# Nineteen of 32 expert groups in the choice stage of an attention and product-key layer, gates from unit 25, one dot a unit

## The chip, the cores and the metric

One core of one Trainium2 chip runs the whole layer. The metric is device time in microseconds (us) from one launch, the median of several runs.

## What is computed

The layer is a hybrid attention block followed by a product-key expert layer (PEER). The change touches the expert layer alone:

```python
T, D = 512, 2048                     # tokens, model width
PEER_HEADS, PEER_TOPK = 8, 16        # 128 chosen experts (slots) a token
q = (xt @ w_pq).reshape(T, PEER_HEADS, 2, PEER_HALF)
s = jnp.einsum('thcd,hcnd->thcn', q, sub_keys)
s1, i1 = lax.top_k(s[:, :, 0], PEER_TOPK)
s2, i2 = lax.top_k(s[:, :, 1], PEER_TOPK)
...
idx = jnp.take_along_axis(cidx, pos, axis=-1)     # 8 x 16 of 16384 experts
g = jax.nn.softmax(top_s, axis=-1)
h = jax.nn.gelu(jnp.einsum('ted,td->te', u[idx], x))
out = jnp.einsum('te,ted->td', g * h, v[idx])
```

All in float32; the tables u and v hold 16384 rows of 2048 numbers each (128 MB a table).

## The kernel before

**Two ways to the same sum.** For tokens 0 to 383 (three blocks, `DB` = 3) the kernel doesn't gather. It multiplies all 16384 rows of u with the tokens, sets to zero by a table of gates what was not chosen, and multiplies with all of v. The last token block (128 tokens, block 3) is computed row by row: for each of its 128 slots one gather of u rows (1 MB, one row a partition), a dot product on the vector engine, later one gather of v rows and one multiply-add (`dot`, L1596, and `add_row`, L1617). The last 48 tokens of block 2 are half and half: their u side is made by 48 gathers and dots (`pair_dot`, L1494: 32 for the last 32 tokens, then 16 for the 16 tokens before them), so the u matmuls have only 336 columns (`UT`), and their v side is dense.

**Units.** Weights come in pieces of 1 MB, called units. For each the DMA queue of SyncE (SP) loads `raw` (`load`, L391), ScalarE (ACT) rounds it to `wh` (`split_hi`, L399), VectorE (DVE) subtracts to get the rest `wl` (`lo`, L1128), and TensorE (PE) multiplies three times, high with high, high with low, low with high (L419 to L421 for u, L444 to L446 for v). There are two buffers of each. The PE's next unit waits for its `lo`; the `split_hi` of unit k waits until PE has finished unit k-2; so `lo` of a unit can start some 2.5 us into the unit before it, and has to be done when that one ends.

**Stages.** The 16384 experts are 32 groups of 4 units of u and 4 units of v (v is cut otherwise, by output columns).
- *Choice stage*: the u units of the first `LAG` = 17 groups, 68 units of index k = 0 to 67. Their results go through gelu to a scratch tensor in DRAM (`act_scratch`, L631), since the gates don't exist yet. Beside these matmuls DVE looks up which experts were chosen (`lookup`, three operations, L1433 to L1440), and from unit `GATE_FROM` = 16 on PE makes the gates: two batches a unit, 96 in all, between the matmuls of the unit (`gate_batch`, L1970), from one-hot tiles that DVE (`hot`, L1456 and L1469) or, for every fourth batch up to number 80, ACT (`rows_act`, L1038 and L1043) has made. ACT copies the batches into `gate_piece` (L1063), and after every eighth SP stores that tile, 2 MB, to DRAM (L662). There is one such tile, so the next copy waits for the store. Each `rows_act` stands behind such copies in ACT's order. The 48 `pair_dot` stand at the units of `DOT_UNITS`; the gather of dot j+2 is issued by GpSimd (POOL, L797) when dot j is done, since there are two row buffers.
- *Main stage*: `NMAIN` = 15 groups with their 4 units of u and then a group's 4 units of v. A group has 5 or 6 slots of block 3 (`SLOT_COUNTS`), each with its dot and its add, and three row buffers: the gather of row n is issued when row n-3 is used (`gather_used`).
- *Tail*: the v units of the other 17 groups, one group alone (set 0) and then eight sets of two groups, 8 units a set. The activations and gates of these groups are read back (L668, L672), multiplied (`gate_mult`, L1584) and split (`tail_w_act` on ACT, L1085, and `tail_rest` on DVE, L1589). The slots of block 3 that are left, 1 and then 5 in each of eight sets, are worked off here.

**Order.** Nothing schedules at run time: each engine's order is written by hand in the loops below, where `for k in range(...)` walks the units. Within a tail set DVE's order is fixed by the source; the adds of the set before are split over two places:

```python
tail_lo(q, 1)
for j in before[:2]:
    add_row(s - 1, j)
tail_lo(q, 2)
gate_mult(NMAIN + 2 * q + 1)
for j in before[2:]:
    add_row(s - 1, j)
dot(s, 0)
tail_chunk(q, 0)
tail_lo(q, 3)
```

`before` is slots 2 and up of the set before (slots 0 and 1 were added at its end), and `tail_chunk` adds a finished output piece from PSUM (L468).

The last 48 tokens' dots come back into the gates by way of `pair_weights` (L1504 and L1509, at unit `DOT_UNITS[-1] + 3`) and a transpose on PE ahead of unit `PAIR_TURN` (`turn_pair`, L1960).

Of the kernel before, what the change touches and what calls it, by code (L numbers as in the profile page):

```python
# [47 lines left out]
GRP = 4  # L48
NGRP = NKEYS // GRP
CH = D // 512  # L50
LAG = 17
DB = TB - 1
TD = DB * P
PT = 32
PB = 16
UT = TD - PT - PB
FULL = UT // 32
PQ = P // PT
NMAIN = NGRP - LAG
GT = 32  # L60
NGC = TD // GT
GATE_FROM = 16
GATE_STEP = 2
GATE_UNITS = DB * 32 // GATE_STEP
GATE_PARTS = (2, 5)
LOOK_ORDER = (2, 0, 1, 3)
LOOK_AT = {1: GATE_FROM, 3: GATE_FROM + 38}
TURN_AT = (13, GATE_FROM + 12, GATE_FROM + 28)
PAIR_TURN = GATE_FROM + 40
GM = 6  # L70
SLOTS = PH * TOPK
PN = SLOTS // PQ
# [1 line left out]
assert GATE_STEP == 2  # L74
QB = P // PB
NB = SLOTS // QB
DOT_UNITS = sorted([8, 9, 11, 12, 13, 14, 15] + list(range(20, 39)) + list(range(21, 38, 3)) +
                   list(range(40, 52)) + list(range(42, 52, 3)))
assert len(DOT_UNITS) == PN + NB and DOT_UNITS[PN - 1] == 38 and DOT_UNITS[PN] == 40
assert GATE_FROM == 16 and UT % 16 == 0 and FULL == UT // GT and PAIR_TURN < GATE_FROM + (SLOTS - PB - PT) // 4 + 32  # L80
EPS = 1e-6
SQ_ACT = (0, 2, 3)
SCALE = float(HD) ** -0.5
# [8 lines left out]
N_PRO = N_PQ + 2 * PH  # L92
N_MAIN = N_PRO + GRP * LAG
N_TAIL = N_MAIN + 2 * GRP * NMAIN
N_END = N_TAIL + GRP * LAG
N_PROUNITS = GRP * LAG
LO_DVE = N_PRO + 4
# [4 lines left out]
M_PRO = M_PQ + 2 * PH  # L102
M_MAIN = M_PRO + GRP * LAG

# [4 lines left out]
FC = 40  # L109
TAIL_SETS = [(0,)] + [(_r, _r + 1) for _r in range(1, LAG, 2)]  # L110
SET_START = [sum(CH * len(_q) for _q in TAIL_SETS[:_n]) for _n in range(len(TAIL_SETS))]
# [28 lines left out]
def build(nc, x, attn_g, w_f, w_in, b_forget, q_g, k_g, w_out, ffn_g, ffn_row, w_pq, sub_keys, u, v, u_rows,  # L140
          v_rows, out):
    ctx = ExitStack()
    with ctx:
# [979 lines left out]
        def _(dve):  # L1123
# [302 lines left out]
            def lookup(t, c, half):  # L1426

                s0 = t * P + 64 * half
                look3 = look.rearrange("p (s j) -> p s j", j=TOPK)
                look4 = look.rearrange("p (h k j) -> p h k j", h=PH // 2, k=TOPK)  # L1430
                if t == DB:
                    dve.wait_ge(slots_turned, 1)
                picked(nc.vector.tensor_tensor(  # L1433
                    look3, pos2f[c][:, s0:s0 + 64].unsqueeze(2).broadcast_to([P, 64, TOPK]),
                    iota16[:].unsqueeze(1).broadcast_to([P, 64, TOPK]), ALU.is_equal))
                picked(nc.vector.tensor_tensor(
                    look4, look4.bitcast(F32),
                    idx_f[:, t, 4 * half:4 * half + 4, c, :].unsqueeze(2).broadcast_to([P, PH // 2, TOPK, TOPK]),
                    ALU.mult))
                nc.vector.tensor_reduce(slots[t][:, c, 64 * half:64 * half + 64], look3.bitcast(F32), AX.X,  # L1440
                                        ALU.add).then_inc(slots_done, 1)
                dve.wait_ge(slots_done, 4 * LOOK_ORDER.index(t) + 2 * c + half + 1)
# [92 lines left out]
            for k in range(8, GATE_FROM):  # L1535
                lo(N_PRO + k + 1)
                if k < 12:
                    lookup(0, (k - 8) // 2, (k - 8) % 2)
                if k == TURN_AT[0]:
                    take_slots(0)  # L1540
                for j, at_unit in enumerate(DOT_UNITS):
                    if at_unit == k:
                        pair_dot(j)
            hot(0)
            hot(1)
            for k in range(GATE_FROM, N_PROUNITS):
                ahead = GATE_STEP * (k - GATE_FROM) + 2
                lo(N_PRO + k + 1)
                if ahead < DB * 32:
                    hot(ahead)  # L1550
                for t in (1, DB):
                    if LOOK_AT[t] <= k < LOOK_AT[t] + 4:
                        lookup(t, (k - LOOK_AT[t]) // 2, (k - LOOK_AT[t]) % 2)
                for j, at_unit in enumerate(DOT_UNITS):
                    if at_unit == k:
                        pair_dot(j)
                if k == 20:
                    dve.wait_ge(side_chosen, 16 * QB)
                    nc.vector.memset(p_h[P // 2:P - PT], 1.0).then_inc(side_one, 1)
                if k == DOT_UNITS[-1] + 3:  # L1560
                    pair_weights()
                if ahead + 1 < DB * 32:
                    hot(ahead + 1)
                for t in range(1, DB):
                    if k == TURN_AT[t]:
                        take_slots(t)
                if k == PAIR_TURN:
                    take_pair()
                if k == LOOK_AT[DB] + 4:
                    nc.vector.scalar_tensor_tensor(out=g_idx[:], in0=slots[DB][:, 0, :], scalar=float(NKEYS),  # L1570
                                                   in1=slots[DB][:, 1, :], op0=ALU.mult,
                                                   op1=ALU.add).then_inc(chosen_done, 1)
                if k == GATE_FROM + GATE_UNITS:
                    nc.vector.memset(stat[:, 15:16], 0.0).then_inc(choice_done, 1)
# [512 lines left out]
```

## Time and profile before

| | us |
|---|---|
| median of 3 runs | 3251.55 (3249.18 to 3255.22) |
| the profiled execution, its own time | 3252.24 |
| its span, first to last instruction | 3250.5 |
| mean granted TensorE clock | 0.998 |
| PE busy | 3216.1 (99%) |
| DVE busy | 2263.4 (70%; 87% in the main stage, 83% in the tail) |
| ACT, POOL busy | 1119.1, 933.6 |
| choice stage | 1153 to 1756 |
| main stage | 1756 to 2691 |
| tail | 2691 to 3247 |

The span is the time between the first and the last recorded instruction, 1.7 us less than the execution's own time. Times in rows are counted from the span's start. A page of the profile gives the busy time of each engine, and a matmul's mean there overlaps with its neighbours; the pace of PE is read from the starts of instructions. An idle time in brackets at the end of a timeline row is that of the row's engine just before it, with the instruction or transfer that ended it.

### The profile page before, as it was taken

To read this page: it belongs to the slowest core of one execution; us is meant where nothing else is said; L and a number is where in the kernel's file an instruction comes from. 1 tells how busy PE (TensorE), PEld (TensorE's weight loads), DVE (VectorE), ACT (ScalarE), POOL (GpSimd) and SP (SyncE) were. 2 spreads that over 40 slices of the span, in tenths; PEclk is the share of its full clock that TensorE was granted. 3 is DMA by queue.
4 is the path that set the end of the run, shared out by engine and by line. 5 is a ranking of instruction groups with operands and counts; after the bars stand their busy time and mean duration, and the time that the engine had idled before them with its cause. 6 is when DMAs were issued, how large, how long until landed. Compare 5 with 4: busy or idle time off the path is not lost. (4 is left out here: it accounts for less than half of the span.)

```text
span 3250.5 us, 41510 instructions
## 1 busy us (share of the span) xinstructions
PE 3216.1 (99%) x16730; PEld 2818.6 (87%) x16730; DVE 2263.4 (70%) x2636; ACT 1119.1 (34%) x1172; POOL 933.6 (29%) x424
## 2 busy tenths in 40 slices
PE   8999999999999999999999999999999999999999
PEld 6878778887878899999999899889989988888887
DVE  5666541113027888887874888888889888888887
ACT  5232323334232233655553223223222322222221
POOL 4333333333434321111101323223322321223222
PEclk9999999999999999999999999999999999999999
DMA  3222222223233247889877989999989998888888
GB/s 144 78 78 90 77 78 78 78 78 141 92 116 121 88 161 255 304 316 318 311 243 265 352 333 352 336 341 345 358 332 335 350 343 312 320 336 340 343 319 317
DMA packets 171364, 777.87 MB, mean 239 GB/s; under 512 B 14064, under 2 KB 80752, under 8 KB 86384
## 3 DMA queue, kind: packets, MB, share of 16 engines
q1 hardware_dynamic: 127488, 457.77, 38.6%
q0 software_dynamic: 43776, 318.79, 26.3%
q8 instruction: 60, 0.98, 0.1%
q14 instruction: 40, 0.33, 0.0%
HBM read 731.10 MB, written 44.34 MB: 239 GB/s over the span
## 5 line engine op out<-in xcount | busy, mean ns | idle before, releaser
L419 PE MATMUL bank<-xh,wh 128*128 128x336 f32 (+1 forms) x3184 | 1105.8, 347 | 1.6 <-DVE wl L1128 1.6
L421 PE MATMUL bank<-xh,wl 128*128 128x336 f32 (+1 forms) x3184 | 1090.1, 342 | 0.0
L420 PE MATMUL bank<-xl,wh 128*128 128x336 f32 (+1 forms) x3184 | 1088.2, 342 | 0.0
L399 ACT ACTIVATE wh<-raw 128x2048 fp32r<-128x2048 f32 x344 | 658.0, 1913 | 999.0 <-PE bank L446 723.3
L1128 DVE TENSOR_TENSOR wl<-raw,wh 128x2048 fp32r<-128x2048 f32 x252 | 576.8, 2289 | 215.2 <-ACT wh L399 214.9
L419 PEld LDWEIGHTS bank<-xh,wh 128*128 128x128 f32 x3184 | 599.3, 188 | 46.5 <-issue 3.8
L420 PEld LDWEIGHTS bank<-xl,wh 128*128 128x128 f32 x3184 | 599.5, 188 | 44.7 <-issue 1.9
L421 PEld LDWEIGHTS bank<-xh,wl 128*128 128x128 f32 x3184 | 598.2, 188 | 45.1
L405 POOL TENSOR_TENSOR wl<-raw,wh 128x2048 fp32r<-128x2048 f32 x92 | 424.9, 4618 | 739.5 <-ACT wh L399 739.5
L444 PE MATMUL bank<-wh,xh 128*128 128x512 f32 x1072 | 417.1, 389 | 0.8 <-DVE stat L1302 0.8
L446 PE MATMUL bank<-wh,xl 128*128 128x512 f32 x1072 | 417.0, 389 | 0.0
L445 PE MATMUL bank<-wl,xh 128*128 128x512 f32 x1072 | 417.0, 389 | 0.0
L811 POOL DMA_INDIRECT arena<-in_u_rows,g_idx x128 | 249.3, 1947 | 456.2 <-DVE acc L1617 224.5
L811 POOL DMA_INDIRECT arena<-in_v_rows,g_idx x128 | 179.2, 1400 | 605.3 <-DVE acc L1617 317.3
L1596 DVE CUSTOM_DVE_ANT_0 arena<-arena 128x2048 f32<-128x2048 f32 x128 | 291.9, 2288 | 54.9 <-DMA arena<-in_u_rows,g_idx 54.8
L1617 DVE SCALAR_TENSOR_TENSOR acc<-arena,acc 128x2048 f32<-128x2048 f32 x128 | 300.5, 2347 | 3.5 <-DMA arena<-in_v_rows,g_idx 0.2
L444 PE MATMUL bank<-wh,gh 128*128 128x512 f32 x720 | 280.6, 390 | 1.6 <-DVE wl L1128 1.6
L446 PE MATMUL bank<-wh,gl 128*128 128x512 f32 x720 | 280.3, 389 | 0.0
L445 PE MATMUL bank<-wl,gh 128*128 128x512 f32 x720 | 280.2, 389 | 0.0
L444 PEld LDWEIGHTS bank<-wh,xh 128*128 128x128 f32 x1072 | 201.2, 188 | 42.8 <-DVE stat L1302 1.0
L445 PEld LDWEIGHTS bank<-wl,xh 128*128 128x128 f32 x1072 | 201.2, 188 | 41.8
L446 PEld LDWEIGHTS bank<-wh,xl 128*128 128x128 f32 x1072 | 201.2, 188 | 41.6
(211 smaller groups left out, 2803.3 us busy)
## 6 DMA issues: line engine op xcount, KB each, us to landing
raw<-in_u SPq DMA_DIRECT2D x128, 1024.0 KB, 5.8
raw<-in_v SPq DMA_DIRECT2D x128, 1024.0 KB, 6.2
raw<-in_w_in SPq DMA_DIRECT2D x56, 1024.0 KB, 4.8
gate_scratch<-arena SPq DMA_DIRECT2D x12, 2048.0 KB
arena<-gate_scratch SPq DMA_DIRECT2D x32, 768.0 KB, 9.0
raw<-in_w_out SPq DMA_DIRECT2D x16, 1024.0 KB, 4.9
raw<-in_w_pq SPq DMA_DIRECT2D x16, 1024.0 KB, 4.9
act_scratch<-arena SPq DMA_DIRECT2D x68, 168.0 KB, 4.4
```

The lines of the kernel that those rows point to most:

```text
L399: nc.scalar.activation(wh[s][:], raw[s][:], ACT.Copy).then_inc(hi_done, 1)
L405: nc.gpsimd.tensor_tensor(wl[s][:], raw[s][:], wh[s][:].bitcast(F32), ALU.subtract).then_inc(lo_done, 1)
L419: nc.tensor.matmul(dst, w_h[:, c], xh[:, c, 0:width], start=(c == 0), stop=False)
L420: nc.tensor.matmul(dst, w_h[:, c], xl[:, c, 0:width], start=False, stop=False)
L421: last = nc.tensor.matmul(dst, w_l[:, c], xh[:, c, 0:width], start=False, stop=(c == KC - 1))
L444: nc.tensor.matmul(bank[:], a_hi(e)[:, rows_], w_h[:, e], start=begin, stop=False)
L445: nc.tensor.matmul(bank[:], a_hi(e)[:, rows_], w_l[:, e], start=False, stop=False)
L446: mm = nc.tensor.matmul(bank[:], a_lo(e)[:, rows_], w_h[:, e], start=False, stop=end)
L811: nc.gpsimd.indirect_dma_start(out=rows_g[n % ROW_BUFS], out_offset=None, in_=table, in_offset=bass.IndirectOffsetOnAxis(ap=g_idx[:, slot: ...
L1128: nc.vector.tensor_tensor(wl[k % 2][:], raw[k % 2][:], wh[k % 2][:].bitcast(F32), ALU.subtract).then_inc(lo_done, 1)
L1596: nc.vector.tensor_tensor_reduce(out=rows_g[b], in0=rows_g[b], in1=x_tok, scale=1.0, scalar=0.0, op0=ALU.mult, op1=ALU.add, accum_out=dots ...
L1617: nc.vector.scalar_tensor_tensor(out=acc[:, DB, :], in0=rows_g[b], scalar=dots[:, GM + j:GM + j + 1], in1=acc[:, DB, :], op0=ALU.mult, op1 ...
```

## The change

`LAG` becomes 19, so the choice stage has 76 units and the main stage 13 groups; the tail has set 0 and nine sets of two groups. `GATE_FROM` becomes 25, so the gates are made in units 25 to 72 instead of 16 to 63, with three units behind them instead of four. The lookup of block 1 moves to units 14 to 17, ahead of the gates. `DOT_UNITS` is another list: 16 dots before unit 25 (units 18, 21 and 24 have two), then one in each of units 25 to 43 but 30, 36 and 42, and one in each of 45 to 61 but 52. From `LAG` follow the slots: 76 in the main stage, 1 in set 0, then 6 in each of six tail sets and 5 in each of three.

```diff
-LAG = 17
+LAG = 19
...
-GATE_FROM = 16
+GATE_FROM = 25
...
-LOOK_AT = {1: GATE_FROM, 3: GATE_FROM + 38}
+LOOK_AT = {1: 14, 3: GATE_FROM + 38}
...
-DOT_UNITS = sorted([8, 9, 11, 12, 13, 14, 15] + list(range(20, 39)) + list(range(21, 38, 3)) +
-                   list(range(40, 52)) + list(range(42, 52, 3)))
+DOT_UNITS = sorted([8, 10, 12, 13, 14, 16, *range(18, 25), 18, 21, 24] +
+                   [_k for _k in range(25, 44) if _k not in (30, 36, 42)] +
+                   [_k for _k in range(45, 62) if _k != 52])
...
                 if k < 12:
                     lookup(0, (k - 8) // 2, (k - 8) % 2)
+                if LOOK_AT[1] <= k < LOOK_AT[1] + 4:
+                    lookup(1, (k - LOOK_AT[1]) // 2, (k - LOOK_AT[1]) % 2)
...
-                for t in (1, DB):
-                    if LOOK_AT[t] <= k < LOOK_AT[t] + 4:
-                        lookup(t, (k - LOOK_AT[t]) // 2, (k - LOOK_AT[t]) % 2)
+                if LOOK_AT[DB] <= k < LOOK_AT[DB] + 4:
+                    lookup(DB, (k - LOOK_AT[DB]) // 2, (k - LOOK_AT[DB]) % 2)
...
-                if k == 20:
+                if k == GATE_FROM + 4:
```

In the changed file lines from 1541 on stand two higher and those from 80 to 1540 one higher.

**DVE ahead of the first gate batch**: before (units 14 and 15, then the one-hot tiles of batches 0 and 1); `L1494` is a dot, whose second row reads its sum.

```order
L1128 TENSOR_TENSOR wl<-raw,wh 128x2048
L1494 ISA acc,arena<-acc 128x2048
L1494 ISA arena 128x1
L1128 TENSOR_TENSOR wl<-raw,wh 128x2048
L1494 ISA acc,arena<-acc 128x2048
L1494 ISA arena 128x1
L1456 TENSOR_TENSOR gh<-iota,arena 128x512
L1464 TENSOR_SCALAR arena<-arena 128x128
```

The same place in the changed kernel (units 23 and 24):

```order
L1129 TENSOR_TENSOR wl<-raw,wh 128x2048
L1495 ISA acc,arena<-acc 128x2048
L1495 ISA arena 128x1
L1129 TENSOR_TENSOR wl<-raw,wh 128x2048
L1495 ISA acc,arena<-acc 128x2048
L1495 ISA arena 128x1
L1495 ISA acc,arena<-acc 128x2048
L1495 ISA arena 128x1
L1457 TENSOR_TENSOR gh<-iota,arena 128x512
L1465 TENSOR_SCALAR arena<-arena 128x128
```

The last unit ahead of the gates now has two dots in front of the first one-hot tile, where it had one.

**DVE in a tail set**, from the `lo` of its second unit to that of its fourth: before.

```order
L1128 TENSOR_TENSOR wl<-raw,wh 128x2048
L1617 SCALAR_TENSOR_TENSOR acc<-arena,acc 128x2048 x2
L1128 TENSOR_TENSOR wl<-raw,wh 128x2048
L1584 TENSOR_TENSOR arena<-arena 128x4x12x32
L1617 SCALAR_TENSOR_TENSOR acc<-arena,acc 128x2048
L1596 ISA arena<-arena 128x2048
L1596 ISA arena 128x1
L468 TENSOR_TENSOR acc<-bank,acc 128x3x512
L1128 TENSOR_TENSOR wl<-raw,wh 128x2048
```

And in the changed kernel, in tail sets 2 to 7 (whose set before has 6 slots):

```order
L1129 TENSOR_TENSOR wl<-raw,wh 128x2048
L1619 SCALAR_TENSOR_TENSOR acc<-arena,acc 128x2048 x2
L1129 TENSOR_TENSOR wl<-raw,wh 128x2048
L1586 TENSOR_TENSOR arena<-arena 128x4x12x32
L1619 SCALAR_TENSOR_TENSOR acc<-arena,acc 128x2048 x2
L1598 ISA arena<-arena 128x2048
L1598 ISA arena 128x1
L469 TENSOR_TENSOR acc<-bank,acc 128x3x512
L1129 TENSOR_TENSOR wl<-raw,wh 128x2048
```

Between two `lo` there is one more add; the third row that is `lo` has to be done before the same end of a unit as before.

**SP at the end of the choice stage**: before, from the last store of gates to the first loads for the main stage.

```order
L662 DMA gate_scratch<-arena 128x32x128
L391 DMA raw<-in_u 128x2048
L631 DMA act_scratch<-arena 128x336
L391 DMA raw<-in_u 128x2048
L631 DMA act_scratch<-arena 128x336
L668 DMA arena<-act_scratch 128x4x336
L672 DMA arena<-gate_scratch 128x1536
L391 DMA raw<-in_u 128x2048
```

And in the changed kernel:

```order
L663 DMA gate_scratch<-arena 128x32x128
L392 DMA raw<-in_u 128x2048
L632 DMA act_scratch<-arena 128x336
L669 DMA arena<-act_scratch 128x4x336
L673 DMA arena<-gate_scratch 128x1536
L392 DMA raw<-in_u 128x2048
```

One load and one store of results stand between the last store of gates and the read of it, where two pairs stood: it is one unit nearer to the main stage.

## Rows read from the trace of the kernel before

**Rows 1.** The page: busy us of each engine, share of the span, instructions.

```profile
PE 3216.1 (99%) x16730; PEld 2818.6 (87%) x16730; DVE 2263.4 (70%) x2636; ACT 1119.1 (34%) x1172; POOL 933.6 (29%) x424
```

**Rows 2.** Timeline of ACT in the choice stage, the gelu at each unit's start (start, us, engine, line).

```profile
1634.62 0.45 ACT L1029 ACTIVATE arena<-bank 128x336 f32<-128x336 f32 x1 [1.15 <-PE bank L421]
...
1741.32 0.45 ACT L1029 ACTIVATE arena<-bank 128x336 f32<-128x336 f32 x1 [5.11 <-PE bank L421]
1748.68 0.45 ACT L1029 ACTIVATE arena<-bank 128x336 f32<-128x336 f32 x1 [4.38 <-PE bank L421]
```

**Rows 3.** Timeline of PE: where it waited between the choice stage's first gate and the main stage.

```profile
1276.55 0.49 PE L1970 MATMUL bank<-arena,gh 128*128 128x128 f32 x2 [0.36 <-ACT arena L1043]
...
1408.57 0.85 PE L1970 MATMUL bank<-arena,gh 128*128 128x128 f32 x3 [3.00 <-ACT arena L1043]
...
1521.38 0.49 PE L1970 MATMUL bank<-arena,gh 128*128 128x128 f32 x2 [0.78 <-ACT arena L1043]
...
1562.10 0.79 PE L1970 MATMUL bank<-arena,gh 128*128 128x128 f32 x3 [3.43 <-ACT arena L1043]
...
1764.95 0.41 PE L419 MATMUL bank<-xh,wh 128*128 128x336 f32 x1 [1.58 <-DVE wl L1128]
```

**Rows 4.** One stretch by engine: busy us (instructions), then PE's granted clock, DMA share, GB/s.

```profile
1408.80:1412.20 3.40, 3.40 (x15) 3.40 (x15) 1.52 (x1) 3.40 (x4) 0.00 (x0) 0.50 0.31 123
```

**Rows 5.** Timelines of SP, POOL and ACT around two stores of gates.

```profile
1388.40 0.39 SPq L662 DMA_DIRECT2D gate_scratch<-arena  x1
1430.56 0.39 SPq L662 DMA_DIRECT2D gate_scratch<-arena  x1
...
1385.72 0.94 POOL L797 DMA_INDIRECT acc<-in_u_rows,arena  x1 [0.30 <-issue]
...
1403.88 2.05 ACT L1063 ACTIVATE arena<-bank 128x512 f32<-128x512 f32 x2 [7.96 <-DMA gate_scratch<-arena]
1440.12 2.13 ACT L1063 ACTIVATE arena<-bank 128x512 f32<-128x512 f32 x2 [2.65 <-DMA gate_scratch<-arena]
```

**Rows 6.** Timeline of DVE after unit 15's dot: the first tile of batch 0.

```profile
1272.81 0.69 DVE L1456 TENSOR_TENSOR gh<-iota,arena 128x512 fp32r<-128x512 f32 x1
```

**Rows 7.** Timelines of DVE and ACT at unit 55: the pair's weights, and the unit's gelu.

```profile
1645.34 0.29 DVE L1509 TENSOR_TENSOR arena<-arena 64x128 f32<-64x128 f32 x1
...
1643.79 0.45 ACT L1029 ACTIVATE arena<-bank 128x336 f32<-128x336 f32 x1 [4.96 <-PE bank L421]
```

**Rows 8.** Timelines of POOL, SP and ACT ahead of the main stage.

```profile
1739.96 0.26 POOL L804 MEMSET arena<- 128x192 f32 x1 [131.02 <-DMA gate_scratch<-arena]
...
1742.29 0.37 SPq L668 DMA_DIRECT2D arena<-act_scratch  x1
...
1760.51 1.92 ACT L399 ACTIVATE wh<-raw 128x2048 fp32r<-128x2048 f32 x1 [4.01 <-DMA raw<-in_u]
```

**Rows 9.** Timeline of DVE in the fifth two-group tail set.

```profile
2990.47 4.80 DVE L1617 SCALAR_TENSOR_TENSOR acc<-arena,acc 128x2048 f32<-128x2048 f32 x2
...
2999.88 2.35 DVE L1617 SCALAR_TENSOR_TENSOR acc<-arena,acc 128x2048 f32<-128x2048 f32 x1
3003.51 2.29 DVE L1596 CUSTOM_DVE_ANT_0 arena<-arena 128x2048 f32<-128x2048 f32 x1 [1.28 <-DMA arena<-in_u_rows,g_idx]
...
3005.72 1.75 DVE L468 TENSOR_TENSOR acc<-bank,acc 128x1536 f32<-128x1536 f32 x1
3007.39 2.28 DVE L1128 TENSOR_TENSOR wl<-raw,wh 128x2048 fp32r<-128x2048 f32 x1
```

**Rows 10.** PE, POOL at that place; the last row is from the chain of waits.

```profile
3010.11 0.39 PE L444 MATMUL bank<-wh,xh 128*128 128x512 f32 x1
...
2984.50 3.00 POOL L811 DMA_INDIRECT arena<-in_v_rows,g_idx  x1 [7.27 <-DVE acc L1617]
...
2993.08 3.00 POOL L811 DMA_INDIRECT arena<-in_u_rows,g_idx  x1 [4.34 <-DVE acc L1617]
...
2519.17 11.07 DMA arena<-in_u_rows,g_idx
```

More of the change, by code:

```diff
@@ L76 @@
 NB = SLOTS // QB
-DOT_UNITS = sorted([8, 9, 11, 12, 13, 14, 15] + list(range(20, 39)) + list(range(21, 38, 3)) +
-                   list(range(40, 52)) + list(range(42, 52, 3)))
-assert len(DOT_UNITS) == PN + NB and DOT_UNITS[PN - 1] == 38 and DOT_UNITS[PN] == 40
-assert GATE_FROM == 16 and UT % 16 == 0 and FULL == UT // GT and PAIR_TURN < GATE_FROM + (SLOTS - PB - PT) // 4 + 32
+DOT_UNITS = sorted([8, 10, 12, 13, 14, 16, *range(18, 25), 18, 21, 24] +
+                   [_k for _k in range(25, 44) if _k not in (30, 36, 42)] +
+                   [_k for _k in range(45, 62) if _k != 52])
+assert len(DOT_UNITS) == PN + NB and DOT_UNITS[PN - 1] == 43 and DOT_UNITS[PN] == 45
+assert UT % 16 == 0 and FULL == UT // GT and DOT_UNITS[-1] + 3 < PAIR_TURN <= GATE_FROM + 40
 EPS = 1e-6
```

## The prediction, made before the changed kernel ran

> **What bounds the kernel now.** I read the page first: PE is busy for 99% of the span [rows 1], so time can come and go only where PE waits or runs at another pace. The number of matmuls of each shape is the same before and after: two groups move from the main stage to the tail, their u units to the choice stage, and the 96 gate batches stay 96. So I looked for pace and for waits. The pace is even: from the gelu of one unit to the next it is 1748.68 - 1741.32 = 7.36 us for a u unit without gates [rows 2] and 1643.79 - 1634.62 = 9.17 us with two gate batches [rows 2, 7]; neither price changes when a unit moves. The waits are few [rows 3]: at the gate batches PE was idle for 0.36, 3.00, 0.78 and 3.43 us because ACT's rows (L1043) were late, and for 1.58 us in the second main unit because `lo` was. After the wait of 3.00 us PE's granted clock was 0.50, the lower of its two levels (1.2 of 2.4 GHz), for 3.4 us [rows 4]; half of that, 1.7 us, is lost on top. I take the same behind the wait of 3.43.
>
> Why was ACT late? At unit 28 SP issued a store of gates at 1388.40, and ACT could make its next copy at 1403.88, 15.5 us later, after 7.96 us of idling; the next store took 1440.12 - 1430.56 = 9.6 us and PE did not wait [rows 5]. Units 27 and 28 have three dots, so a gather had just been issued (1385.72) and others followed [rows 5]. With 15.5 us PE was idle for 3.00, so a store of up to some 12.5 us is hidden.
>
> **The change, part by part.**
>
> *One dot a unit: minus 10.6.* Since a dot's end issues the next gather, single dots 9.17 us apart leave at most one gather before a store and one during it, as around the store of 9.6 us (units 31 to 33). No store should pass 12.5 us then. What goes: 3.00 + 1.7, 3.43 + 1.7 and 0.78 = 10.6 us [rows 3, 4]. Bounds: 9 (a stall of one or two us stays) to 11.
>
> *The first gate: plus 5.0.* Batch 0 needs the tile that DVE makes behind the last dot. From that point (1272.81) to PE's batch (1276.55) it took 3.74 us, ACT's rows in between, and it came 0.36 too late [rows 3, 6]. Now unit 24 has two dots ahead of it. `lo` starts 2.5 us into the unit, behind gelu (0.45) and `split_hi` (1.92) [rows 2, 8], and takes 2.3, a dot takes 3005.72 - 3003.51 = 2.2 [rows 9], so DVE is free 9.2 us after the unit's start and batch 0 ready at 12.9; it is due at 7.36 + 2.8 (18 matmuls) = 10.2. Idle: 2.7 us at the least. The last dot's gather also has to come: it is issued when the dot of unit 23 ends (7.0 us into it), and from a gather's issue to its use pass 8.4 to 11.1 us (tail, below), which makes that dot 1.0 to 3.7 us later. I take 2.7 + 1.0 = 3.7, with the clock's 1.7, less the 0.36 of before: 5.0. Bounds: 2.3 (no late gather, no lower clock) and 7.7. The lookups moved to units 14 to 17 cost nothing: block 0's stand in the same way with `lo` and dots in units 8 to 11, before and now, and PE did not wait there.
>
> *The pair's weights: plus 1.2.* They are made in the unit `DOT_UNITS[-1] + 3`: before 54, while the transpose stands ahead of unit 56; now 64, with the transpose ahead of unit 65. Before, DVE had them at 1645.34 + 0.29 = 1645.6, and unit 55 had begun 0.35 us before its gelu, at 1643.4: 2.2 us earlier [rows 7]. Two units' room hid that. Now PE waits; the batch made in unit 64 is one whose rows ACT makes, so DVE has four small one-hot operations less ahead of the weights, by my guess 1 us. Bounds 1.0 and 2.2; I take 1.2.
>
> *The way into the main stage: plus 2.* The main stage's first loads wait for the last store of gates (POOL sees it at 1739.96), then read activations and gates (1742.29) and only then fetch the second main unit, which reached ACT at 1760.51, 20.5 us after the store; that made the wait of 1.58 [rows 3, 8]. The store is now one unit of 7.36 us nearer, so the wait could become 9 us. Against that, SP's read was held until 1742.29 by the result of unit 65, 2.3 us behind the store, and now isn't; and it comes level with POOL's first three gathers instead of behind them. Bounds minus 0.3 and plus 7.4; I take 2, nearer the low end because the read now leads. The Trainium skill (DMA: Bandwidth & Descriptors, Queues, rings and completion order) says that a DMA engine takes turns between queues packet by packet, so that neither SP's read nor POOL's gathers would block the other; by that rule the early read loses little and this term would be 0.5, the sum 1.5 lower. No row shows the turns.
>
> *The tail: plus 18.* This is the costly part. `LAG` = 19 leaves 51 slots for nine sets, and six have 6 where all had 5. The sixth adds a dot and an add. Two slots' adds come at the end of a set and two behind the second unit's start, so the additional add stands between the `lo` of the third and of the fourth unit, in six sets. In the fifth set of two groups of before, this stretch ended with the `lo` at 3007.39 + 2.28 = 3009.67, and PE began the next unit at 3010.11: 0.44 us of room [rows 9, 10]. The dot before it had waited 1.28 us for its gather. An add costs 2.27 us more in a row of adds (two take 4.80, overlapping by their ends [rows 9]). Without any wait for a gather: 3009.67 - 1.28 + 2.27 = 3010.66, so PE is some 0.6 to 0.8 us late. With it: the first dot of a set uses the row buffer freed by the slot three before, which with 6 slots is the add ending at 2990.47 + 4.80 = 2995.27 [rows 9]. Its gather is issued behind that of 2993.08, which keeps POOL for 3.00, so at 2996.4 [rows 10]. From issue to use passed 3003.51 - 2993.08 = 10.4 us here and 11.07 in the densest place of the main stage; and at most 8.4 where the add in the pair from 2990.47 on used the gather of 2984.50 without a wait [rows 9, 10]. With 10.4 the dot starts at 3006.8, and then 3009.67 - 3003.51 = 6.2 us follow: 3013.0, 2.9 us late. With 11.07 it is 3.6, and 4.1 if the adds before slip too; with 8.4 the adds decide and it is 0.8. Since every set's first `lo` is tied to PE by its `split_hi`, the lateness comes anew in each set: six times. I take 3.0, by the row of this very place: 18 us; bounds 6 x 0.7 = 4 and 6 x 4.1 = 25. Main groups with 6 slots show that the pattern stands more elsewhere: there `dot`s are spread over five units.
>
> *At nothing:* the end of the main stage now has a group with 6 slots ahead of set 0, with one add more before the second `lo`; I find 1 us of room left by the same walk. The 3 MB of `acc` read back for blocks 0 to 2 are issued behind unit 65's store and have three units until the next. The 2 us of small waits for gathers in the main stage stay.
>
> **Sum:** -10.6 + 5.0 + 1.2 + 2 + 18 = +15.6 us. The profiled execution's own time was 3252.2, 0.7 above the median 3251.55; the sum is put on the median: **3267**.
>
> **Rivals.**
> - *The clock goes down in the tail too (3277).* With 3 us each, the tail's waits are about as long as those of 3.00 us, behind which the granted clock was 0.50 [rows 3, 4]. Six times 1.7 is 10 more. For it: the length. Against: most of the six would have to reach it, and my bounds begin at 0.7. The Trainium skill (TensorE: Matmul & The Clock Gate, HAM oscillation) describes just this, idle stretches inside a loop that put PE back to 1.2 GHz time after time.
> - *Gathers come in time in the tail (3254).* With some 8.4 us from issue to use the tail costs 0.8 a set: 5 instead of 18, so +2.6. For it: the dots of the other tail sets did not hold up their `lo`, and the gathers that matter are issued at the same points as before. Against: the waiting dot of [rows 9].
> - *Faster (3244).* DVE's room covers the add, so the tail costs nothing; the first gate costs its least (2.3), the pair 1.0, the way into the main stage 0: -10.6 + 3.3 = -7.3. It decides whether one add fits between the two `lo`: 2.27 against 0.44 + 1.28 = 1.72 us. It misses by 0.55, by rows of a single set.
> - *The stores stay slow (3278).* Single dots still put gathers ahead of a store, because with two buffers there is nearly always one under way, and the stalls of 10.6 us stay. Against: the 9.6 us store had single dots around it.
>
> **How the numbers follow.** Chances: my sum 0.52, the clock 0.18, slow stores 0.08, gathers in time 0.14, faster 0.08. A measurement of this kernel tells about 0.2% (6.5 us) from no change. The first three are slower by more than that: 0.78. Gathers in time is within it: 0.14. The last is faster: 0.08. All lower bounds together give 3248, all upper ones 3285, and they won't fall together; the range is 3252 to 3284, which leaves out the faster case, the lower part of the fourth, and the upper part of the second.
>
> **What would show it.** In the choice stage no wait of PE on L1043 beyond the first gate, and there one of about 4 us; no wait of ACT on the gate store above 4 us before unit 61. A wait of a bit over 1 us at the transpose of the pair (L1962 in the changed file). In the second main unit a wait of 2 to 5 us. In the tail six waits of about 3 us on `lo`, 65 us apart plus the wait, behind a dot that waited for u rows. I am wrong if the tail stays without waits, or if the stores still take 15 us.

## The result: 1.0% slower, twice what was forecast

| | before | after |
|---|---|---|
| median of 5 runs, us | 3252.73 (3249.18 to 3258.18) | 3285.26 (3283.3 to 3288.97) |
| ratio, 95% interval | 1 | 1.010 (1.0086 to 1.0114) |
| profiled execution, its own time | 3252.24 | 3285.26 |
| its span | 3250.5 | 3283.5 |
| mean granted TensorE clock | 0.998 | 0.994 |

The forecast was 3267, with a range to 3284: the direction is right, the time 1.3 us outside the range, and the loss 32.5 us instead of 15.6.

The page of the changed kernel, the line of [rows 1] and three groups of instructions (busy, mean ns | idle before, releaser):

```profile
PE 3227.1 (98%) x16730; PEld 2824.9 (86%) x16730; DVE 2259.8 (69%) x2631; ACT 1120.1 (34%) x1171; POOL 927.9 (28%) x424
...
L445 PE MATMUL bank<-wh,xh 128*128 128x512 f32 x1168 | 460.1, 394 | 27.1 <-DVE wl L1129 26.3
...
L1598 DVE CUSTOM_DVE_ANT_0 arena<-arena 128x2048 f32<-128x2048 f32 x128 | 291.4, 2288 | 67.9 <-DMA arena<-in_u_rows,g_idx 67.7
L1619 DVE SCALAR_TENSOR_TENSOR acc<-arena,acc 128x2048 f32<-128x2048 f32 x128 | 300.6, 2349 | 9.6 <-DMA arena<-in_v_rows,g_idx 6.1
```

The same 16730 matmuls are busy 11 us longer (the granted clock is lower, see below), and the v units waited 26.3 us for `lo` (27.1 us is all the idle time before these matmuls). Where, the timeline of PE shows; first the three waits outside the tail that answer to [rows 3], then all six of the tail:

```profile
1345.84 0.88 PE L1972 MATMUL bank<-arena,gh 128*128 128x128 f32 x3 [3.67 <-ACT arena L1044]
...
1713.51 0.33 PE L1962 MATMUL bank<-ident,arena 128*128 128x128 f32 x1 [0.97 <-DVE arena L1510]
...
1817.91 0.42 PE L420 MATMUL bank<-xh,wh 128*128 128x336 f32 x1 [1.03 <-DVE wl L1129]
...
2747.17 0.80 PE L445 MATMUL bank<-wh,xh 128*128 128x512 f32 x1 [4.45 <-DVE wl L1129]
...
2819.56 0.79 PE L445 MATMUL bank<-wh,xh 128*128 128x512 f32 x1 [4.43 <-DVE wl L1129]
...
2890.44 0.50 PE L445 MATMUL bank<-wh,xh 128*128 128x512 f32 x1 [3.25 <-DVE wl L1129]
...
2960.80 0.80 PE L445 MATMUL bank<-wh,xh 128*128 128x512 f32 x1 [4.76 <-DVE wl L1129]
...
3033.09 0.79 PE L445 MATMUL bank<-wh,xh 128*128 128x512 f32 x1 [5.27 <-DVE wl L1129]
...
3105.51 0.79 PE L445 MATMUL bank<-wh,xh 128*128 128x512 f32 x1 [4.10 <-DVE wl L1129]
```

The places are those of the forecast: the first gate (3.67), the pair (0.97), the second main unit (1.03, before 1.58), and six times the fourth unit of a tail set, 26.3 us in all. The waits of 3.00, 0.78 and 3.43 at the gates [rows 3] are gone. The duration in the second column tells the clock: five of the six matmuls behind a wait show 0.79 or 0.80 us, the one behind 3.25 shows 0.50. The stretches behind those waits (PE, weight load, DVE, ACT, POOL busy; then the granted clock, as in [rows 4]):

```profile
2745.40:2752.20 6.80, 5.03 (x12) 3.97 (x13) 6.80 (x4) 0.00 (x0) 0.00 (x0) 0.51 0.95 348
2817.00:2823.80 6.80, 4.24 (x10) 3.37 (x11) 6.80 (x5) 0.13 (x1) 0.00 (x0) 0.51 0.90 317
2886.80:2893.60 6.80, 3.55 (x16) 2.61 (x15) 6.80 (x4) 1.91 (x1) 0.92 (x1) 1.00 0.97 365
2960.40:2963.80 3.40, 3.00 (x7) 2.42 (x8) 3.40 (x3) 0.00 (x0) 0.00 (x0) 0.52 0.99 361
3032.10:3038.90 6.80, 5.81 (x14) 4.55 (x15) 6.80 (x4) 0.00 (x0) 0.00 (x0) 0.51 0.95 373
3103.80:3110.60 6.80, 5.09 (x12) 4.02 (x13) 6.80 (x4) 0.00 (x0) 0.00 (x0) 0.51 0.93 359
```

In the five stretches at 0.51 or 0.52 (1.2 of 2.4 GHz) PE was busy for 5.03 + 4.24 + 3.00 + 5.81 + 5.09 = 23.2 us; half of that, 11.6, is what the clock cost.

A table of stage lengths, from the starts of each unit's last matmul, is used below. The columns are units; without a wait, unit 25 takes 9.17 us, the 56 units 195 to 250 take 457.0 and the rest 40.8. (The kernels with an e are the experiments of the next section.) Each row is a single execution.

| profiled execution | unit 25 | 26 to 64 | 65 | 77 | 78 to 194 | 195 to 250 | rest |
|---|---|---|---|---|---|---|---|
| after | 14.69 | 358.4 | 10.69 | 8.67 | 917.1 | 496.1 | 40.8 |
| e1 sixth add and dot behind `lo` | 19.73 | 358.4 | 10.69 | 8.40 | 915.7 | 459.6 | 45.6 |
| e9 only the dot behind `lo` | 17.27 | 358.4 | 10.68 | 9.45 | 916.7 | 457.2 | 40.8 |
| e4 sixth add on 64 columns | 20.54 | 358.4 | 10.68 | 9.26 | 920.1 | 495.7 | 41.0 |
| e2 four sets of six | 16.17 | 358.4 | 10.67 | 8.43 | 918.2 | 483.9 | 40.8 |
| e5 dots and pair moved | 9.79 | 358.4 | 9.29 | 11.24 | 919.2 | 497.9 | 42.2 |
| e11 only the dot of unit 24 moved | 9.78 | 358.4 | 10.69 | 9.44 | 917.5 | 496.9 | 41.9 |
| e8 e1 and e5, and the last set | 9.79 | 358.4 | 9.29 | 9.31 | 917.8 | 459.0 | 40.8 |
| e12 e8 with the pair late | 9.79 | 358.4 | 10.69 | 9.36 | 918.8 | 458.4 | 40.8 |
| e10 e8 with doubled dots | 11.19 | 371.8 | 9.29 | 9.75 | 918.7 | 459.2 | 40.8 |

Before, units 195 to 250 took 457.0. The tail alone is +39.1.

### The profile page after: what moved, and what is told of

Read it like the earlier page. It is cut to its first block and busy times, and to the rows that moved or that the text cites. A ratio compares the mean times of both kernels' runs of the same rounds, so it can differ in the third digit from the quotient of the medians.

```text
span 3283.5 us, 41419 instructions
## 1 busy us (share of the span) xinstructions
PE 3227.1 (98%) x16730; PEld 2824.9 (86%) x16730; DVE 2259.8 (69%) x2631; ACT 1120.1 (34%) x1171; POOL 927.9 (28%) x424
## 5 line engine op out<-in xcount | busy, mean ns | idle before, releaser
L445 PE MATMUL bank<-wh,xh 128*128 128x512 f32 x1168 | 460.1, 394 | 27.1 <-DVE wl L1129 26.3
L446 PE MATMUL bank<-wl,xh 128*128 128x512 f32 x1168 | 458.6, 393 | 0.0
L447 PE MATMUL bank<-wh,xl 128*128 128x512 f32 x1168 | 458.3, 392 | 0.0
L812 POOL DMA_INDIRECT arena<-in_u_rows,g_idx x128 | 227.1, 1775 | 419.6 <-DVE arena L1598 222.2
L445 PEld LDWEIGHTS bank<-wh,xh 128*128 128x128 f32 x1168 | 222.2, 190 | 75.9 <-DVE wl L1129 28.8
L446 PEld LDWEIGHTS bank<-wl,xh 128*128 128x128 f32 x1168 | 222.1, 190 | 46.4
L447 PEld LDWEIGHTS bank<-wh,xl 128*128 128x128 f32 x1168 | 221.8, 190 | 46.7
L445 PE MATMUL bank<-wh,gh 128*128 128x512 f32 x624 | 243.4, 390 | 0.5 <-DVE wl L1129 0.3
L447 PE MATMUL bank<-wh,gl 128*128 128x512 f32 x624 | 242.9, 389 | 0.0
L446 PE MATMUL bank<-wl,gh 128*128 128x512 f32 x624 | 242.9, 389 | 0.0
```

The lines of the kernel that those rows point to most:

```text
L445: nc.tensor.matmul(bank[:], a_hi(e)[:, rows_], w_h[:, e], start=begin, stop=False)
L446: nc.tensor.matmul(bank[:], a_hi(e)[:, rows_], w_l[:, e], start=False, stop=False)
L447: mm = nc.tensor.matmul(bank[:], a_lo(e)[:, rows_], w_h[:, e], start=False, stop=end)
L812: nc.gpsimd.indirect_dma_start(out=rows_g[n % ROW_BUFS], out_offset=None, in_=table, in_offset=bass.IndirectOffsetOnAxis(ap=g_idx[:, slot: ...
```

## The experiments

Each was compared with the kernel before on its own chip; the medians of before were 3250.9 (e1 to e4), 3252.0 (e5, e6, e8, e9) and 3253.96 (e10 to e12), so across these groups the ratios count.

**e3: before with LAG = 19 alone.** It separates the split of the groups from the gates and dots.

```diff
-LAG = 17
+LAG = 19
```

> The kernel before with LAG = 19 alone: gates from unit 16 and the old list of dots stay. Theory (the changed list gives 11 us in the choice stage, and its two new waits, at the first gate and at the pair's transpose, take 6.3): the tail's 39 us are there, the two waits at ACT's rows are back, the new ones are not, and the last store of gates is far from the main stage, whose first wait goes too: 3252 + 39 - 2 = 3289, some 4 us above the changed kernel. Rival (the choice stage's list makes the tail's waits, through the phase of the gathers): no waits in the tail, about 3250.

Measured 3289.3, ratio 1.0115 (1.0098 to 1.0132). Units 195 to 250 took 496.5 us, 39.5 over, as in the changed kernel (39.1). `LAG` makes the whole loss. Whether the gates and dots take a little of it back can't be told: the intervals of the two ratios overlap, and the profiles are 4.1 us apart. The old list's stalls were there again, but at units 30 and 34 (9.4 us together) instead of 30 and 46.

**e2: four sets of six instead of six.** Two of the 51 tail slots go to the main stage.

```diff
-SLOT_COUNTS = [GM - (_r % 5 == 4) for _r in range(NMAIN)]
+SLOT_COUNTS = [GM for _r in range(NMAIN)]
```

> The changed kernel, with 6 slots in every group of the main stage, so that four tail sets have 6 slots instead of six. Theory (each tail set behind one with 6 slots costs some 6.5 us): four waits instead of six, 13 us less, 3272, and nothing more than 1 us in the main stage. Rival (all tail sets cost, by more traffic): the same time, 3285, or more, since the main stage becomes denser by two slots and its two waits of about 1 us become four.

Measured 3278.63, ratio 1.0089 (1.0072 to 1.0106). Units 195 to 250: 483.9, so four sets cost 26.9 us, 6.7 each, where six cost 39.1, 6.5 each. The four sets behind six slots had a wait, and sets 6 and 7, now behind five, had none: the cost goes with the number of sets behind six slots, as forecast. The time shows less of it: by the ratios (1.0089 against 1.0100) 3.6 us of the 12.2 that the stage shows, with intervals that overlap, and not the 3272 that I expected; in the profile unit 25 took 1.5 and the main stage 1.1 us more.

**e1: the sixth add and the set's first dot behind `lo`.**

```diff
-                for j in before[2:]:
+                late = len(before) > 3
+                for j in before[2:3] if late else before[2:]:
                     add_row(s - 1, j)
-                dot(s, 0)
+                if not late:
+                    dot(s, 0)
                 tail_chunk(q, 0)
                 tail_lo(q, 3)
+                if late:
+                    add_row(s - 1, before[3])
+                    dot(s, 0)
```

> The changed kernel, with the sixth add of the set before and the first dot moved behind the lo of the fourth unit, in the six tail sets whose set before has 6 slots. Theory (the added time is the tail's: a lo that stands behind a waiting dot is late, six times 3.4 to 5.4 us of waiting, and the lower clock behind each): the dot's wait for its gather, some 3.5 us, now falls where the next lo is not due for 9 us, so none of the six waits is left, the clock stays up, and all 39 us go: 3246, about 6 us below the kernel before. Rival (the tail's gathers are short of bandwidth, and where they wait is a matter of place): the waits move to the lo of the fifth unit and 10 to 30 us stay.

Measured 3253.52 (10 runs), ratio 1.0008 (0.9998 to 1.0017): some 30 us of the loss are gone, and it is still 7 us above the 3246 that I expected. The six waits disappeared (the 56 units are 2.6 us over the undisturbed length); 4.8 us came up in a new place, the fourth unit of the last set (the rest took 45.6 instead of 40.8 us), where two dots stand ahead of that `lo`. Unit 25 was 5 us longer than in the changed kernel's profile, with the same code.

**e4 and e9: the add or the dot?** My sum went by the dot's gather; its lower bound, and the rivals "gathers in time" and "faster", went by the add's own time. e4 makes the sixth add small (64 of 2048 columns, the others of that row are left out) and changes nothing in the order.

```diff
+                cols = slice(0, 64 if r > NMAIN and j == 5 else D)
-                nc.vector.scalar_tensor_tensor(out=acc[:, DB, :], in0=rows_g[b],
-                                               scalar=dots[:, GM + j:GM + j + 1], in1=acc[:, DB, :],
+                nc.vector.scalar_tensor_tensor(out=acc[:, DB, cols], in0=rows_g[b][:, cols],
+                                               scalar=dots[:, GM + j:GM + j + 1], in1=acc[:, DB, cols],
```

> The changed kernel, with the sixth add of a tail set on 64 of 2048 columns (the output of the last token block is short of it); its gather is unchanged. Theory A (the late gather of the first dot decides; it is issued when the add two places ahead ends, so the sixth add's own 2.3 us lie inside the dot's wait of 3.3 to 3.8 us): the waits of PE stay within 0.3 us of what they were, the dot waits 2.2 us longer, total within 2 us of 3285. Theory B (my prediction's lower bound: the vector engine's own time decides): each of the six waits is 2.2 us shorter and the clock drops less, 13 to 25 us faster.

One execution, 3297.4. That is neither figure, but the stage table tells the two theories apart: units 195 to 250 took 495.7 us, 0.4 less than in the changed kernel (theory A). The 12 us more lie outside the edit: 5.9 in unit 25, 2.3 ahead of the choice stage, some 3.6 in units 77 to 194, 0.6 ahead of unit 25. DVE in its second such set:

```profile
2817.59 2.35 DVE L1620 SCALAR_TENSOR_TENSOR acc<-arena,acc 128x2048 f32<-128x2048 f32 x1
2820.60 0.28 DVE L1620 SCALAR_TENSOR_TENSOR acc<-arena,acc 128x64 f32<-128x64 f32 x1 [0.67 <-DMA arena<-in_v_rows,g_idx]
2825.89 2.29 DVE L1598 CUSTOM_DVE_ANT_0 arena<-arena 128x2048 f32<-128x2048 f32 x1 [5.00 <-DMA arena<-in_u_rows,g_idx]
```

The add took 0.28 us instead of 2.35, and the dot behind it waited 5.00 us for its gather where it had waited 3.26 in the changed kernel. So the add's duration is not on the path; the dot's row is.

e9 moves the dot alone, and leaves the whole sixth add ahead of `lo`:

```diff
                 for j in before[2:]:
                     add_row(s - 1, j)
-                dot(s, 0)
+                late = len(before) > 3
+                if not late:
+                    dot(s, 0)
                 tail_chunk(q, 0)
                 tail_lo(q, 3)
+                if late:
+                    dot(s, 0)
```

> The changed kernel with only the first dot of a six-slot set moved behind the chunk and lo of the third unit; all six adds stay ahead. Theory G: it is the dot's gather that holds lo up (its buffer comes free at the end of the fourth add, and free to landed takes 11 us; the sixth add ends 3.0 us after the unit's end, well ahead). Then lo ends at 3.0 + 1.7 + 2.3 = 7.0 us of the 8.16 us unit, the six waits go, and the time is that of the kernel with both moved, 3253 (3249 to 3257). Theory S, that of the prediction: the sixth add is what does not fit, and with it still ahead of lo about half of the loss stays: 3262 to 3272.

Measured 3253.98 (10 runs), ratio 1.0015 (1.0003 to 1.0028); units 195 to 250 took 457.2, the undisturbed length. The ten executions scatter from 3248.70 to 3265.92, more than any other kernel's here, and the profile is of one of the shortest (3249.22); what the long ones did isn't known. DVE at the place of the former first wait:

```profile
2737.81 2.35 DVE L1619 SCALAR_TENSOR_TENSOR acc<-arena,acc 128x2048 f32<-128x2048 f32 x1 [0.30 <-DMA arena<-in_v_rows,g_idx]
2740.08 1.75 DVE L469 TENSOR_TENSOR acc<-bank,acc 128x1536 f32<-128x1536 f32 x1
2741.75 2.28 DVE L1129 TENSOR_TENSOR wl<-raw,wh 128x2048 fp32r<-128x2048 f32 x1
2744.26 2.29 DVE L1598 CUSTOM_DVE_ANT_0 arena<-arena 128x2048 f32<-128x2048 f32 x1 [0.23 <-DMA arena<-in_u_rows,g_idx]
```

With the sixth add in front, chunk and `lo` follow at once; the dot comes behind them and waits 0.23 us for the same row. Theory G stands, theory S falls. The expectation calls S that of the prediction; it is that of its lower bound, while the 18 us were walked by G.

**e6: are three dots in a row what makes a gate store slow?** Before, with three dots moved by one unit.

```diff
-DOT_UNITS = sorted([8, 9, 11, 12, 13, 14, 15] + list(range(20, 39)) + list(range(21, 38, 3)) +
-                   list(range(40, 52)) + list(range(42, 52, 3)))
+DOT_UNITS = sorted([8, 9, 11, 12, 13, 14, 15] + list(range(20, 39)) + [21, 24, 26, 30, 33, 36] +
+                   list(range(40, 52)) + [41, 46, 48, 51])
```

> The kernel before with three of its 23 extra or paired dots moved by one unit (27 to 26, 42 to 41, 45 to 46), so that no three dots stand in a row ahead of the unit whose gate store was slow (15.5 us and 9.6 us). Theory of the prediction: the stores of the waiting units 30 and 46 are slow because of the gathers that the extra dots issue beside them; moving the dots shifts or removes these two waits (4.9 and 5.3 us of unit length): 3241 to 3246. Rival: the store is slow whatever the neighbouring dots do, as the gathers come one to a dot anyway: 3249 to 3253.

Measured 3250.43 (10 runs), ratio 0.9997 (0.9986 to 1.0008): no gain. The waits moved to units 30, 34 and 50 (2.6, 6.9 and 6.6 us longer). But the trace shows that the edit hadn't removed what I suspected: at the slow stores a gather was still issued just ahead (2.1, 3.5 and 3.6 us). The better sign is SP's next instruction behind the store, the issue of a load: it took 7.4, 9.2 and 7.1 us there, and 4.4 to 5.5 at the other stores made while dots were running.

**e10: gathers put ahead of the stores on purpose.** The other way round, in the kernel without such waits (e8, below):

```diff
-                   [_k for _k in range(25, 44) if _k not in (36, 42)] +
+                   [25, 26, 27, 28, 28, 29, 31, 32, 32, 33, 35, 36, 36, 37, 40, 40, 43] +
```

> The kernel that beats both (e8, 3246.8) with four dots of the choice stage doubled at units 28, 32, 36 and 40, the units ahead of those with a gate store, and as many later single ones left out (35, 37.. to 43 thinned). In eight profiles the transfer that SP issues behind a gate store took 4.7 to 5.9 us where no gather had been issued in the 3.6 us ahead of the store, with one exception, and 6.0 to 9.2 us where one had. Theory: the doubled dots put a gather there, three or four stores become slow, and PE waits at one to three of the units behind them, 3 to 5 us each with the clock's loss: 3252 to 3262. Rival: the slow stores of the kernel before came of something else in its stage, and the time stays within 2 us of 3246.8.

Measured 3261.74, ratio 1.0026 (1.0015 to 1.0037), against 0.998 without the doubles: 0.46%, 15 us. Units 26 to 64 took 371.8 instead of 358.4. SP, POOL and ACT around the second store, and then the same for the changed kernel's first store:

```profile
1423.27 0.39 SPq L663 DMA_DIRECT2D gate_scratch<-arena  x1
1424.13 10.35 SPq L392 DMA_DIRECT2D raw<-in_u  x1
...
1421.37 0.94 POOL L798 DMA_INDIRECT acc<-in_u_rows,arena  x1 [0.30 <-issue]
...
1439.22 1.96 ACT L1064 ACTIVATE arena<-bank 128x512 f32<-128x512 f32 x2 [8.74 <-DMA gate_scratch<-arena]
```

```profile
1385.88 0.40 SPq L663 DMA_DIRECT2D gate_scratch<-arena  x1
1386.33 4.82 SPq L392 DMA_DIRECT2D raw<-in_u  x1
...
1380.14 1.15 POOL L798 DMA_INDIRECT acc<-in_u_rows,arena  x1 [7.01 <-DVE arena L1495]
1390.34 0.94 POOL L798 DMA_INDIRECT acc<-in_u_rows,arena  x1 [9.04 <-DVE arena L1495]
...
1394.11 2.15 ACT L1064 ACTIVATE arena<-bank 128x512 f32<-128x512 f32 x2 [1.03 <-DMA gate_scratch<-arena]
```

A gather 1.9 us ahead of the store: 16.0 us until ACT can copy again. The nearest gathers 5.7 us ahead and 4.5 us behind: 8.2 us.

**e5 and e11: the first gate and the pair.** e5 takes the second dot out of unit 24 and ends the list a unit earlier; e11 does the first alone.

```diff
-DOT_UNITS = sorted([8, 10, 12, 13, 14, 16, *range(18, 25), 18, 21, 24] +
-                   [_k for _k in range(25, 44) if _k not in (30, 36, 42)] +
-                   [_k for _k in range(45, 62) if _k != 52])
+DOT_UNITS = sorted([8, 10, 12, 13, 14, 16, *range(18, 25), 18, 21] +
+                   [_k for _k in range(25, 44) if _k not in (36, 42)] +
+                   list(range(45, 61)))
```

> The changed kernel with one edit: a single dot at choice unit 24 instead of two, the dot put at unit 30 instead, and the second list at units 45 to 60, so that the pair's weights fall in unit 63, not 64. Theory: the first gate (unit 25) waits 4.0 us and makes the unit 5.5 us longer in the changed kernel's profile (8.3 and 9.7 us of wait in two other profiles of the same stage) because the second dot of unit 24 waits for its gather and stands ahead of the gate's one-hots on VectorE; and the turn of the pair (unit 65) is 1.5 us longer because the weights are one unit late. Then both go: first gate's wait under 1 us, pair's 0, and the time 3285 - 5.5 - 1.5 = 3278, down to 3273 if most executions have the longer wait. Rival: the first gate waits for something that the dots do not set (gh's first build, the table load on ScalarE), and the time stays at 3284 to 3286.

> The changed kernel with the second dot of unit 24 moved to unit 30 and nothing else (the pair's weights stay in unit 64). With the pair moved too the profile showed 6 us won in the choice stage, but 2.6 us lost again at the way into the main stage, where the 3 MB read of acc then stood ahead of a gate store (SP's issue behind it took 10.8 us, not 4.6), and 5 us lost in the main stage and the tail. Theory: it was the pair's turn that gave it back; without it the time is 3285 less 5 to 8: 3277 to 3280. Rival: in the changed kernel the gain of the first gate is lost whatever the pair does, and the time stays at 3284 to 3288.

Measured: e5 3286.55, ratio 1.0106 (1.0091 to 1.0122); e11 3284.44, ratio 1.0098 (1.0083 to 1.0113); the changed kernel itself 1.0100. Both did in their place what was expected: the wait of PE on L1044 is 0.4 us instead of 3.67, unit 25 takes 9.8 us, and in e5 the pair's wait is gone. The time did not follow. By the stage table e11 gave back 0.8 in unit 77, 0.4 in the main stage, 0.8 in units 195 to 250 and 1.1 in the rest; e5 2.6, 2.1, 1.8 and 1.4. Theory "the pair gives it back" fell with e11. Whether a real coupling or the scatter of so few executions (their intervals reach down to 3 and 5.5 us below the changed kernel's median ratio) eats the gain is open. One part has a place: the 1.1 and 1.4 us in the rest are a wait in the fourth unit of the last set, as in e1, which is where the last edit of e8 is made.

**e8 and e12: the version that beats both.** e8 is e1 and e5 together, and in the last set the second dot goes behind `lo` as well:

```diff
             dot(s, 0)
-            dot(s, 1)
             tail_chunk(q, 0)
             tail_lo(q, 3)
-            dot(s, 2)
+            dot(s, 1)
             tail_lo(q, 4)
-            for j in range(3, ns):
+            for j in range(2, ns):
                 dot(s, j)
```

> The version that should beat both: the changed kernel with the tail's first dot and sixth add behind lo (3253.5 measured for that alone), the dots of the choice stage moved as in the run before, and in the last set of the tail the second dot behind lo as well (its wait was 3.3 us, the unit 3.8 us longer, in the profile of that kernel). Theory: the costs add up, one place each: 3253.5 less 5 to 10 for the first gate, 1.5 for the pair, 3.4 for the last set: 3241, range 3237 to 3244. Rival: what is taken away comes back at the next wait (VectorE is 90% busy in the tail), and the time stays at 3247 or more.

Measured 3246.79 (11 runs, 3241.16 to 3250.41), ratio 0.998 (0.9971 to 0.9989): 0.2% faster than before and 1.2% faster than the change. Its list of PE's waits (us in total, times, longest) names for the stages at hand:

```profile
PE bank L445 <- DVE wl L1129: 3.3, 5, 1.4
PE bank L420 <- DVE wl L1129: 1.7, 1, 1.7
```

It missed my 3237 to 3244 by 3 us. Here the first gate's gain seems to have held: e9 has nearly the same tail, and stands at 1.0015. No run isolates it, since e8 differs from e9 in the tail's order and the pair too.

e12 is e8 with the second list of dots left as in the change:

```diff
-                   list(range(45, 61)))
+                   [_k for _k in range(45, 62) if _k != 52])
```

> The kernel that beats both (e8, 3246.8) with the second list of dots as in the changed kernel, so that the pair's weights come in unit 64 and the read of acc stands behind the gate store, as in the run before. Theory: the wait at the pair (1.5 us) comes back and the way into the main stage gets 1 to 2.6 us shorter: 3244 to 3247. Rival: only the pair's wait comes back: 3248 to 3249.

Measured 3249.25 (12 runs), ratio 0.9989 (0.998 to 0.9999). Unit 77 was no shorter (9.36 against 9.31), so the theory falls; the rival is nearer, and the intervals of the two overlap.

## Why the prediction was wrong, point by point

| term | forecast | between the two profiles |
|---|---|---|
| single dots | -10.6 | -11.3 |
| first gate | +5.0 | +4.9 |
| the pair's weights | +1.2 | +1.4 |
| way into the main stage | +2 | -0.5 |
| tail | +18 | +39.1 |
| sum | +15.6 | +33.6 |

The measured column is the lengthening of the units: before 4.85 (unit 30), 0.12 (34), 1.04 (42) and 5.29 us (46) at the gates that went, 0.62 at the old first gate and 0.12 at the pair; after 5.52 (unit 25) and 1.52 (65). The way into the main stage is 1.03 less 1.58. The profiled executions are 33.0 us apart.

**The tail was mis-sized.** The mechanism, the place and the number of waits were right: six waits on `lo`, each behind a dot that waits for its gather. The step that failed is "I take 3.0, by the row of this very place: 18 us", together with the clock, which I had put among the rivals. DVE and POOL in the first such set, to be laid beside [rows 9, 10]:

```profile
2723.80 4.80 DVE L1619 SCALAR_TENSOR_TENSOR acc<-arena,acc 128x2048 f32<-128x2048 f32 x2
...
2732.40 4.80 DVE L1619 SCALAR_TENSOR_TENSOR acc<-arena,acc 128x2048 f32<-128x2048 f32 x2
2740.95 2.29 DVE L1598 CUSTOM_DVE_ANT_0 arena<-arena 128x2048 f32<-128x2048 f32 x1 [3.75 <-DMA arena<-in_u_rows,g_idx]
...
2743.16 1.75 DVE L469 TENSOR_TENSOR acc<-bank,acc 128x1536 f32<-128x1536 f32 x1
2744.83 2.28 DVE L1129 TENSOR_TENSOR wl<-raw,wh 128x2048 fp32r<-128x2048 f32 x1
```

```profile
2726.42 2.99 POOL L812 DMA_INDIRECT arena<-in_v_rows,g_idx  x1 [5.20 <-DVE acc L1619]
2729.72 1.90 POOL L812 DMA_INDIRECT arena<-in_u_rows,g_idx  x1 [0.30 <-issue]
```

The buffer is free at 2723.80 + 4.80 = 2728.60, POOL issues at 2729.72, and the dot starts 11.2 us later, at 2740.95; I had taken 10.4. PE was ready for the next unit at 2742.56, 0.23 us behind its last matmul of the unit, and got its `lo` 4.6 us later. In the row of before, 14.84 us lay between the free buffer and PE's start (3010.11 - 2995.27); here 2742.56 - 2728.60 = 13.96. So 2.9 by my walk, 0.9 because the adds stand later against PE, and 0.8 from the gather: 4.6. I had written this case down ("and 4.1 if the adds before slip too") and made it a bound, though the sixth slot is what makes them slip: the second add of that pair ends 14.6 us ahead of the third unit's last matmul in sets 2 to 7 of before and in set 8 here, which stands behind five slots, and only 13.0 to 14.0 us ahead in the six sets behind six.

The gather was priced by the wrong row. The 10.4 us belong to the gather of 2993.08 [rows 10], issued 5.3 us behind the one ahead of it. The gather that decides in the changed kernel is issued about 3.3 us behind another, and before that is the place of the second one, which landed 12.8 us after its issue (the idle of 0.30 shows that it followed at once):

```profile
2996.38 2.72 POOL L811 DMA_INDIRECT arena<-in_u_rows,g_idx  x1 [0.30 <-issue]
```

In the other five sets before, the first of the two landed after 7.4 to 8.8 us and the second after 9.4 to 11.1. In the six sets of the changed kernel the deciding one took 10.2 to 12.3, and the shortest and the longest belong to the waits of 3.25 and 5.27. So 10.4, the longest of six for the wrong gather, came within 0.9 us of the mean of 11.3 by luck. That a gather close behind another lands later is what these rows show; no run changed the distance alone.

The six measured waits have a mean of 4.4: 26.3 us for 18, and 11.6 for the clock. Together 37.9 of the 39.1.

**The clock.** I gave the rival 0.18 and six times 1.7 us. After five of the six waits the granted clock was 0.51 or 0.52, in four of them for twice the 3.4 us of [rows 4], so it cost about 11.6 instead of 10; after the shortest, 3.25 us, it stayed at 1.00. That "my bounds begin at 0.7" was no argument once my own central value was 3.0 and the case at hand had gone down after 3.00 [rows 3, 4]. The Trainium skill (TensorE: Matmul & The Clock Gate, HAM oscillation) describes idle stretches in a loop that put the clock back each time, and the trace agrees, in five sets of six. The other profiles bear it out: of PE's waits of over 2 us from the choice stage on, in all thirteen, the 43 of 3.43 to 9.41 us all went with a stretch at half the clock, and of the eight of 2.07 to 3.25 us three did. With 37.9 us in the place of the 18 the sum gives 3287.

**What else came true.** ACT's wait for the gate store was 1.0 us at the first, no store after unit 25 stopped PE, and e10 shows the cause by bringing it back. The single dots are worth what I said, mostly for the reason that I said, though e6 shows that "three dots in a row" was not the right sign of it. Nor was the store of 9.6 us a model of single dots: unit 33 has two, and POOL had issued a gather 3.4 us ahead of that store. In the changed kernel none is nearer than 5.5 us ahead, and ACT can copy again after 8.0 to 9.2 us. The first gate came out at my 3.7 us of wait (3.67), partly by luck: the same code waited 4.3, 5.1, 8.0 and 9.4 us in the profiles of e2, e9, e1 and e4. The way into the main stage I had at +2; it was -0.5. My estimate by the Trainium skill's rule of turns (DMA: Bandwidth & Descriptors, Queues, rings and completion order) was 0.5, which is nearer; no run shows the turns.

The rival "gathers in time" is refuted by the six waits. The mechanism of "faster" (the add fits) is right in itself, by e9, and of no use while the dot stands in between. (An add with another behind it takes 4.80 - 2.35 = 2.45 us by [rows 9], not my 2.27, which is one with the chunk behind it; nothing rests on the difference.)

## What to carry to other kernels

When a slot is added to a ring of buffers, ask first what the next load waits for: three row buffers and 11.4 to 13.4 us from free to used decided here (10.3 to 12.3 of them from the gather's issue), and the 2.3 us of extra work did not. Price that load by a row in which it stands as close behind its neighbour as it will stand then. A consumer of such a load should stand behind the work that the bounding engine waits for, not ahead of it: one moved dot won 28 us by the ratios (1.0100 to 1.0015). A repeated wait should be costed with the clock's loss on it from the start, if the trace shows the clock going down after one of its length.

## What the runs showed of the chip

- The issue of a load on SP right behind the 2 MB store of gates took 6.0 to 10.4 us in all 13 cases (before, e3, e6, e10) in which POOL had issued a gather 1.4 to 3.6 us ahead of the store. Without one it took 4.3 to 6.2, but for two of 7.0 and 7.5, in thirteen profiles and as long as the dots lasted. A gather issued 4.5 us behind the store stood in both kinds.
- Where the 3 MB read of `acc` is issued 3.4 us ahead of such a store, that issue took 10.8 to 12.5 us (before, e3, e5, e6, e8, e10). In e8 it was 11.1, ACT waited 8.1 us for the store, and PE did not wait; with the read behind the store (e9) it took 4.7.
- Taking away 5 us in the choice stage of the changed kernel (e5, e11) left no difference in the median that can be told; from e9 to e12, without the long waits in the tail, the ratio fell by some 8 us, of which 7.5 can be unit 25 (17.27 and 9.79 us in the profiles); the two differ in the tail's order as well. Why the first gave nothing isn't explained.
